# Splitting GpSimd's low part of the next weight slot in two around four row norms

## The reference, cut to what matters

```python
def rmsnorm(x, gain):
    xf = x.astype(jnp.float32)
    y = xf * lax.rsqrt(jnp.mean(xf * xf, axis=-1, keepdims=True) + EPS)
    ...
        x = x + mix.astype(x.dtype)
        x = x + swiglu(rmsnorm(x, norm_ffn[i]), ffn_w_gate_up[i], ffn_w_down[i]).astype(x.dtype)
```

## Time and profile before

| | |
|---|---|
| median of three runs | 1953.94 us |
| the profiled execution, its own time | 1954.07 us |
| span of its trace (first to last instruction) | 1952.3 us |
| what lies around the span | 1.8 us |
| TensorE matmuls busy | 1908.3 us, 98% |
| GpSimd busy | 828.9 us, 42% |
| of it the splits of line 674 | 145, mean 4624 ns |

### The profile page before, as it was taken

The page is one execution under the profiler, slowest core; times in us unless marked ns, Lnnn a source line. Parts: engine busy times, 40 slices in busy tenths (PEclk is TensorE's granted clock), DMA queues, the critical chain, the costliest instruction groups (busy, mean ns, idle before and its releaser), DMA issues.

```text
span 1952.3 us, 24984 instructions
## 1 busy us (share of the span) xinstructions
PE 1908.3 (98%) x9667; PEld 1542.7 (79%) x9667; DVE 743.9 (38%) x1282; ACT 739.6 (38%) x1141; POOL 828.9 (42%) x414
## 2 busy tenths in 40 slices
PE   7999999999999999999999999999999999999998
PEld 5777888888888878768888888888776778888887
DVE  8883231111002378882311110020546657403721
ACT  6534342232223244683432221243457462212222
POOL 1003344444444458654434344443245444343433
PEclk9899999999999899999999999999999999999999
DMA  6414323333322223102333323335220223323231
GB/s 160 94 27 134 108 84 89 103 91 97 102 94 70 76 72 102 65 2 65 87 107 86 107 75 103 115 87 153 69 65 22 77 60 92 108 86 108 86 108 65
DMA packets 210205, 170.84 MB, mean 88 GB/s; under 512 B 19658, under 2 KB 174746, under 8 KB 210058
## 3 DMA queue, kind: packets, MB, share of 16 engines
q1 hardware_dynamic: 207954, 166.19, 29.0%
q10 hardware_dynamic: 2168, 3.52, 0.5%
HBM read 162.58 MB, written 2.65 MB: 85 GB/s over the span
## 4 chain that ended last, share of the span: by engine, by line
PE 87%; ACT 4%; DVE 3%; issue 2%; SPq 1%; DMA 1%; POOL 1%; POOLq 0%; DVEq 0%; ACTq 0%
PE PS L2169 76%; PE PS L2459 2%; PE PS L2450 2%; PE PS L2469 2%; DMA xp<-in_x 1%; PE PS L2064 1%; SPq L508 1%; PE PS L2065 1%; PE PS L2242 1%; DVE taken L1921 1%; PE PS L2097 1%; PE PS L2412 0%; ACT probs_t L1222 0%; ACT junk L826 0%; ACT u L885 0%
## 5 line engine op out<-in xcount | busy, mean ns | idle before, releaser
L674 POOL TENSOR_TENSOR w_lo<-raw,w_hi 128x2048 fp32r<-128x2048 f32 x145 | 670.5, 4624 | 954.9 <-ACT w_hi L932 838.5
L932 ACT ACTIVATE w_hi<-raw 128x2048 fp32r<-128x2048 f32 x145 | 277.9, 1916 | 629.9 <-PE PS L2169 629.9
L2169 PE MATMUL PS<-xT_hi,w_hi 128*128 128x512 f32 (+1 forms) x1152 | 441.0, 383 | 1.5 <-DVE xT_lo L1605 1.1
L2169 PE MATMUL PS<-xT_lo,w_hi 128*128 128x512 f32 (+1 forms) x1152 | 438.2, 380 | 0.0
L2169 PE MATMUL PS<-xT_hi,w_lo 128*128 128x512 f32 (+1 forms) x1152 | 438.0, 380 | 0.0
L2169 PEld LDWEIGHTS PS<-xT_hi,w_hi 128*128 128x128 f32 x1152 | 216.6, 188 | 47.7 <-issue 6.7
L2169 PEld LDWEIGHTS PS<-xT_lo,w_hi 128*128 128x128 f32 x1152 | 216.6, 188 | 41.6
L2169 PEld LDWEIGHTS PS<-xT_hi,w_lo 128*128 128x128 f32 x1152 | 216.7, 188 | 40.3
L2169 PE MATMUL PS<-w_hi,hT_hi 128*128 128x512 f32 x608 | 236.9, 390 | 0.0
L2169 PE MATMUL PS<-w_hi,hT_lo 128*128 128x512 f32 x608 | 236.6, 389 | 0.0
L2169 PE MATMUL PS<-w_lo,hT_hi 128*128 128x512 f32 x608 | 236.5, 389 | 0.0
(11 more groups left out here) (334 smaller groups left out, 2025.9 us busy)
## 6 DMA issues: line engine op xcount, KB each, us to landing
raw<-in_ffn_w_gate_up SPq DMA_DIRECT2D x88, 512.0 KB, 4.6
raw<-in_ffn_w_down SPq DMA_DIRECT2D x40, 512.0 KB, 4.3
raw<-in_w_up SPq DMA_DIRECT2D x32, 512.0 KB, 5.1
raw<-in_w_down SPq DMA_DIRECT2D x32, 512.0 KB, 4.5
raw<-in_dsa_w_in SPq DMA_DIRECT2D x28, 512.0 KB, 4.5
raw<-in_w_in SPq DMA_DIRECT2D x21, 512.0 KB, 4.3
raw<-in_s_w_glu SPq DMA_DIRECT2D x16, 512.0 KB, 4.5
raw<-in_dsa_w_o SPq DMA_DIRECT2D x8, 512.0 KB, 4.6
```

Source lines behind the costliest of these rows:

```text
L674: pool.tensor_tensor(w_lo[:, par, :], raw[:, par, :], f32(w_hi[:, par, :]), ALU.subtract).then_inc(w_split, 1)
L932: act.activation(w_hi[:, par, :], raw[:, par, :], ACT.Copy).then_inc(w_rounded, 1)
L2169: ins = mm(o, a if weights_stay else c, c if weights_stay else a, start=first and n == 0, stop=last and n == 2)
```

## The change

In `norm_rstd(n)` for n below 4, GpSimd no longer splits the next slot ahead of the row norms in one instruction of 2048 columns. It splits the left 1024 columns first (new semaphore `w_left`), makes the scales of row tiles 0, 1 and 2, splits the right 1024 columns without a wait of its own, and only then raises `w_split` and goes on to row tile 3. The `split_run` calls in front of the four norms are one slot shorter. TensorE waits for `w_left` before the next slot, and for `w_split` ahead of the first product that reads the right columns.

```diff
@@ -296,7 +296,7 @@
 
 
         w_raw = [sem("w_raw0"), sem("w_raw1")]
-        w_rounded, w_split, w_used = sem("w_rounded"), sem("w_split"), sem("w_used")
+        w_rounded, w_split, w_used, w_left = sem("w_rounded"), sem("w_split"), sem("w_used"), sem("w_left")
         t_free, t_first = sem("t_free"), sem("t_first")
         n_free, n_ready = sem("n_free"), sem("n_ready")
         hid_act, hid_hi, hid_done = sem("hid_act"), sem("hid_hi"), sem("hid_done")
@@ -673,22 +673,37 @@
                 pool.wait_ge(w_rounded, g + 1)
                 pool.tensor_tensor(w_lo[:, par, :], raw[:, par, :], f32(w_hi[:, par, :]), ALU.subtract).then_inc(w_split, 1)
 
+            def split_left(g):
+                cols = slice(0, KT * P)
+                pool.wait_ge(w_rounded, g + 1)
+                pool.tensor_tensor(w_lo[:, g % 2, cols], raw[:, g % 2, cols], f32(w_hi[:, g % 2, cols]), ALU.subtract).then_inc(w_left, 1)
+
+            def split_right(g):
+                cols = slice(KT * P, 2 * KT * P)
+                pool.tensor_tensor(w_lo[:, g % 2, cols], raw[:, g % 2, cols], f32(w_hi[:, g % 2, cols]), ALU.subtract).then_inc(w_split, 1)
+
             def split_run(g0, n):
                 for g in range(g0, g0 + n):
                     if g < SLOTS:
                         split_rest(g, g % 2)
 
+            HALVED = (GLU_SLOT + GLU_SLOTS, FFN_SLOT[0] + FT + 2 * len(FFN_DOWN), WO_SLOT + 4, HIN_SLOT)
+
             def norm_rstd(n):
+                if n < 4:
+                    split_left(HALVED[n])
                 pool.wait_ge(row_sq, 2 * TB * n + TB)
                 link(pool.tensor_scalar(rstd[:, 8:8 + TB], ssq[:, 8:8 + TB], 1.0 / D, EPS, ALU.mult, ALU.add))
                 for tb in range(TB):
                     pool.wait_ge(row_sq, 2 * TB * n + TB + tb + 1)
                     link(pool.tensor_scalar(rstd[:, tb:tb + 1], ssq[:, tb:tb + 1], 1.0 / D, rstd[:, 8 + tb:9 + tb], ALU.mult, ALU.add))
                     pool.tensor_tensor(rstd[:, tb:tb + 1], rstd[:, tb:tb + 1], half_neg[:, 0:1], ALU.pow).then_inc(row_rstd, 1)
+                    if n < 4 and tb == 2:
+                        split_right(HALVED[n])
 
 
             pool.wait_ge(s5_x, NB)
-            split_run(0, 1 + GLU_SLOTS)
+            split_run(0, GLU_SLOTS)
             norm_rstd(0)
             split_run(1 + GLU_SLOTS, 1)
 
@@ -698,7 +713,7 @@
                     for j in range(2):
                         split_rest(i * 2 + (g0 + j), (g0 + j) % 2)
                 g0 += FT
-                split_run(g0, 2 * len(FFN_DOWN) - 1)
+                split_run(g0, 2 * len(FFN_DOWN) - 2)
                 norm_rstd(1 + 2 * layer)
                 split_run(g0 + 2 * len(FFN_DOWN) - 1, 1)
 
@@ -771,7 +786,7 @@
 
             split_run(WO_SLOT, 1)
             invert_columns(dsa_units, DSA_UNIT)
-            split_run(WO_SLOT + 1, 4)
+            split_run(WO_SLOT + 1, 3)
             norm_rstd(2)
             split_run(WO_SLOT + 5, 1)
             ffn_split(1)
@@ -2260,7 +2275,7 @@
             def t_slot_halves(g, par, ti, n, j0, freed):
 
                 banks = FIRST_BANKS + LATE_BANKS
-                pe.wait_ge(w_split, g + 1)
+                pe.wait_ge(w_left, n + 1)
                 pe.wait_ge(t_free, ti + 1)
 
                 def tile(t, k, half):
@@ -2271,6 +2286,8 @@
                 for k in range(KT):
                     if k % 2 == 0:
                         pe.wait_ge(x_lo_done, j0 + k // 2 + 1)
+                    if k == KT // 2:
+                        pe.wait_ge(w_split, g + 1)
                     tile(0, k, 0)
                     tile(1, k, 0)
                     if k == 1:
```

## The result

| | before | after |
|---|---|---|
| median of 20 runs each | 1954.87 us | 1958.38 us |
| lowest to highest | 1953.4 to 1956.93 | 1954.86 to 1961.37 |
| the profiled execution, its own time (span) | 1954.07 (1952.3) | 1959.02 (1957.2) |

The ratio is 1.0018 with an interval of 1.0012 to 1.0024: **+3.5 us**, between +2.3 and +4.7. The interval leaves 1 out, so the kernel did become slower, by 0.18%; I had put 83 in 100 on a change of under 0.2% either way. The forecast was +2.5 us and 1956.4 us. The measured 1958.38 lies 2.0 above that and only 0.02 under the upper end of the range, 1958.4: about 1.0 of the 2.0 is the change, and 0.9 is before's own median, which is 1954.87 in 20 runs where three runs had shown 1953.94.

What follows compares the result with a forecast made beforehand. TensorE, busy 98% of the span, was taken as the bound, so only its waits in four norm passages count. 3 x 0.8 + 0.15 = +2.5 us gave a median of 1956.4 us, range 1951.8 to 1958.4.

Steps and rivals of the forecast that it cites:

- The half: GpSimd's split of 1024 columns takes 2.38 us, where the whole split of 2048 takes 4.61.
- Row 0 earlier: Row 0's scale comes 2.2 us earlier, ending TensorE's 0.71 us transpose wait in three passages; first passage 1.32 to about 0.1.
- T: Moment row 2's scale is ready on GpSimd: 0.23 us earlier in three passages, about 1.0 in the first.
- The exclusion: VectorE's fast scaling of row 2 waits out GpSimd's right half, ending at T + 2.73 instead of T + 0.52.
- The next slot: TensorE's next slot waits for `half_lo(0)` behind row 2's scaling and starts at T + 3.68.
- The sum in the passages: Four norm passages: +0.8 us in each of three, +0.15 in the first, +2.5 us in all.
- What was costed at nothing: New `w_split` wait, row 3's scale, SP's load some 6 us later, two more GpSimd instructions per passage: no cost.
- A: VectorE's scaling of row 2 goes first or does not wait for the right half: -1.7 us, 1952.2; chance 0.15.
- B: TensorE's longer stop before the next slot lowers its clock for a spell, losing 6.8 us: 1963; chance 0.05.
- C: All TensorE's waits in the norm passages go, 3.8 us: 1950.1; chance 0.04.

Runs made afterwards that it cites:

- e1: Changed kernel with one more wait: GpSimd starts the right half only after VectorE has scaled row 2's left columns; 1954.07 us, ratio to before 0.9997.
- e8: Changed kernel, but VectorE scales row 2 in the slower form that also keeps a sum nobody reads; 1955.09 us, ratio to before 1.0001.
- e3: Changed kernel with the halves in passage two only, the other three passages as before; 1955.87 us, ratio to before 1.0008.
- e4: Changed kernel with the halves in passages one, three and four, passage two as before; 1955.31 us, ratio to before 1.0007.
- e2: Changed kernel with the right half made straight behind the left one, ahead of the row norms; 1955.34 us, ratio to before 1.0007.
- e5: Kernel of before with slot 44's narrow products 512 columns wide instead of 72; 1959.67 us, ratio to before 1.0026.
- e6: Changed kernel with slot 44's narrow products 512 columns wide instead of 72; 1961.74 us, ratio to before 1.0038.
- e10: Kernel of before with slot 44's narrow products 256 columns wide instead of 72; 1949.80 us, ratio to before 0.9970.
- e11: Changed kernel with slot 44's narrow products 256 columns wide instead of 72; 1951.40 us, ratio to before 0.9981.
- e9: Changed kernel unaltered, measured once more; 1957.59 us, ratio to before 1.0015.
- e7: The kernel of e1 with slot 44's narrow products 512 columns wide instead of 72; 1957.54 us, ratio to before 1.0016.

## Why the prediction was right, and where it was off

- **The half**: 2.38 us forecast, 2.39 measured.
- **Row 0 earlier**: right. The wait at `half_turn` 0 is gone in passages two to four and 0.28 in the first, where I said about 0.1.
- **T**: I had it 0.23 us earlier in the third passage. Taking away what lies ahead of the passage (the add of row 1 stands at 928.60 for 925.09, 3.51 later), T is at 930.24 for 930.45, 0.21 earlier. In the first passage the rounding of slot 8 started 1.18 us later than in before's trace; without that T is at 253.74, 1.03 earlier, for 1.0.
- **The exclusion**: right, and the step that carried the sum. The scaling ends at T + 2.65 (933.79 + 2.61) where T + 2.73 was forecast, by the row at 1385.46 of the earlier trace rows. e1 takes the pair apart and the loss is gone; e8 keeps the pair and changes the form, and it is gone too. So it is shown that this loss needs both: GpSimd's earlier start, and the 0.49 us form of the scaling and not the 0.75 us one.
- **The next slot**: T + 3.68 forecast, 937.33 = T + 3.58 measured. The 0.1 us is the scaling that ends earlier.
- **The sum in the passages**: 3 x 0.8 + 0.15 = 2.5 forecast; 0.71 + 0.75 + 0.72 + 0 = 2.2 measured; e3 and e4 show that the terms add.
- **What was costed at nothing**: the load for the slot after is issued at 936.28, behind the right half, and row 3's squares still find GpSimd idle for 2.52 us (4.34 before). e2 shows that two instructions for one, with nothing between them, cost 0.12 to 0.14 us a passage in three passages and gave 0.20 back in the first.
- **The median**: +3.5, of which 2.2 are the passages. The other 1.3 (0.1 to 2.5 by the interval) lies outside them, and the sum had no term for it. I treated the spell in the earlier trace rows as a price that no change moves, and from slot 44 to 47 it moves the time by up to 3.2 us between kernels that differ only elsewhere; the stretch ahead of slot 1 has another, of 1.7. Two traces cannot say how the 1.3 of the medians divides. With the spell of slot 44 out of the way (e5 against e6, e10 against e11) the difference is 2.1 and 1.6, so nothing is left over.
- **What stays open**: whether the change makes the longer spell likelier, or whether that profile happened on it. This table takes what the passages give away from what the median moved:

  | us | after | e9 | e1 | e2 | e3 | e8 | e4 |
  |---|---|---|---|---|---|---|---|
  | median against before | +3.5 | +2.9 | -0.1 | +1.2 | +1.7 | +0.2 | +1.1 |
  | the four passages | +2.2 | +2.2 | -2.0 | +0.2 | +0.7 | -1.9 | +1.5 |
  | left over | +1.3 | +0.7 | +1.9 | +1.0 | +1.0 | +2.1 | -0.3 |

  Each median is good to 1.2 us (after) or 1.8 us (the others), so no single column decides much. But the six with a changed passage two all have something left over, and e4, the only one that leaves passage two as it was, has not. The mean granted clock of a run says the same, more weakly, since it has three digits and counts every spell: it was 0.991 or less in 12 of the first 20 runs of the changed kernel and 7 of the 11 of e9, in 7 of 11 of e1, 9 of e8, 6 of e3 and 4 of e2, but in 1 of 11 of e4 and 17 of 83 of before. That points to a link between passage two and the spell behind it and does not settle it; no run varies passage two alone in small steps.

The rivals. **A** (VectorE first, or no wait) is refuted for this form: all four scalings waited. Its time is what e1 and e8 reach in the passages, -2.0 and -1.9 for -1.7. **B** (the clock) is refuted where I put it: stops of 1.3 to 1.4 us before the next slot left the clock at 1.00 around all four. The clock did enter, at a place with no stop at all. **C** did not come: TensorE now waits 5.4 us there. That the measured time still lies within the range is in part luck: the passages were 0.3 us better than forecast, what lies outside them 1.3 worse, and before's median 0.9 higher, and all that left 0.02 us to the upper end.

## What to carry to other kernels

Before a long GpSimd instruction is moved to "right behind" a short step, look at what else that step releases: if it is a VectorE instruction in the faster mode on the path that sets the end, GpSimd wins by some hundredths of a us and VectorE waits for all of it; one wait on VectorE's instruction, or the form that keeps a sum, gives the gain that was meant in the passages (the medians of e1 and e8 did not show it; e7's against e5's did). Compare stages by distances between fixed marks of the same engine and not whole executions, and ask of a stage far from the edit that changed whether the granted clock did. Where TensorE's clock is low in a run of narrow products, try them wider, even if the extra columns are thrown away; it paid here with 256 columns and not with 512.

## What the runs showed of the hardware that I had not expected

- A VectorE scaling of 128x512 float32 in SBUF takes 0.49 us alone; 0.07 to 0.08 us behind the start of a GpSimd split of 1024 columns it takes 2.60 to 2.61, and with an accumulated sum 0.75.
- The granted clock fell to 0.50 with TensorE busy for 5.00 of the 5.00 us before it, in a run of 128x72 products, and stayed at 1.00 with products of 256 or 512 columns in the same place. The 96 products with 3.6 times the columns made the stage 5.4 us shorter.
- The length of that spell, 13.7, some 17, or some 20.5 us, moved the same stage between 43.3, 44.9 and 46.5 us in kernels whose code there is the same. Ahead of slot 1 a stretch of 14.1 us at a granted clock of 1.00 took 15.8 in six of fourteen traces, with 0.83 to 0.84 in its later part.
